# Sparse layer of a fused two-block kernel: order of the input projection, rotary halves packed by DMA, index work placed among the query units

## The reference, cut to what matters

```python
def dsa_mixer(h, w_in, w_out, cos_a, sin_a, cos_i, sin_i):
    proj = h @ w_in
    q, k, v, qi, ki, wi = jnp.split(proj, cuts, axis=-1)   # 16, 4, 4 heads of 64; 8, 1 index heads of 64; 8
    q = partial_rope(q, cos_a, sin_a, 16)                  # the first 16 of 64 features are turned
    k = partial_rope(k, cos_a, sin_a, 16)
    qi = partial_rope(qi, cos_i, sin_i, 16)
    ki = partial_rope(ki, cos_i, sin_i, 16)
    wi = wi * IDX_WEIGHT_SCALE
    def block(i):                                          # 64 queries each
        logits = jnp.einsum('bthd,bsd->bths', qib, ki)
        score = jnp.einsum('bths,bth->bts', jax.nn.relu(logits), wib)
        score = jnp.where(visible[None], score, -jnp.inf)
        _, sel = lax.top_k(score, 64)
        ...                                                # k and v gathered, softmax over the selected keys
    return o @ w_out
```

## Time and profile before

| | us |
|---|---|
| median of 3 executions | 1638.37 |
| lowest, highest | 1637.73, 1640.66 |
| the profiled execution | 1634.39 |
| its span in the trace | 1632.5 |
| granted clock of TensorE in it | 0.999 |

### The profile page before, as it was taken

How to read it: one execution, slowest core, us unless ns; L and a number is a source line. 1 busy time by engine, 2 the same in 40 slices (tenths; PEclk the granted TensorE clock), 3 DMA queues, 4 the chain that set the end, 5 groups by cost and what they waited for, 6 DMA issues and landing times.

```text
span 1632.5 us, 30999 instructions
## 1 busy us (share of the span) xinstructions
PE 1590.4 (97%) x12663; PEld 1517.9 (93%) x12663; DVE 1011.2 (62%) x1241; ACT 763.9 (47%) x1005; POOL 23.5 (1%) x40
## 2 busy tenths in 40 slices
PE   7989999998999999999999999999999999999999
PEld 5969999998999998999988999989999898889998
DVE  7786665567666546566457666466654656676653
ACT  4345554447555444434346444344443435554443
POOL 0000000013000000000000000000000000000000
PEclk9999999999999999999999999999999999999999
DMA  6702666744256664556623556635566352236573
GB/s 164 183 31 58 179 201 181 197 141 123 83 179 202 182 195 153 181 166 194 181 77 104 180 177 195 168 113 174 178 195 189 103 181 78 79 129 196 189 213 96
DMA packets 347111, 252.70 MB, mean 155 GB/s; under 512 B 32622, under 2 KB 345868, under 8 KB 347036
## 3 DMA queue, kind: packets, MB, share of 16 engines
q1 hardware_dynamic: 345424, 250.00, 51.4%
q10 hardware_dynamic: 1612, 1.64, 0.3%
HBM read 250.58 MB, written 1.05 MB: 154 GB/s over the span
## 4 chain that ended last, share of the span: by engine, by line
PE 86%; DVE 8%; ACT 3%; DMA 2%; issue 1%; SPq 0%; ACTq 0%; DVEq 0%
PE acc L541 26%; PE acc L543 25%; PE acc L542 25%; DVE w_low L1690 2%; ACT w_high L1199 1%; PE acc L566 1%; PE acc L771 1%; PE spare L739 1%; DMA w_raw<-in_ffn_w_dram 1%; PE acc L757 1%; DVE x_state L1900 1%; DVE xg_low L1734 1%; DVE evac_a L1898 1%; PE spare L604 1%; PE spare L566 1%
## 5 line engine op out<-in xcount | busy, mean ns | idle before, releaser
L1690 DVE TENSOR_TENSOR w_low<-w_raw,w_high 128x2048 fp32r<-128x2048 f32 (+2 forms) x222 | 528.5, 2381 | 378.3 <-ACT w_high L1199 378.3
L1199 ACT ACTIVATE w_high<-w_raw 128x2048 fp32r<-128x2048 f32 (+2 forms) x222 | 441.3, 1988 | 612.0 <-PE acc L543 578.3
L541 PE MATMUL acc<-xg_high,w_high 128*128 128x272 f32 (+2 forms) x2320 | 663.4, 286 | 7.6 <-DVE xg_low L1734 4.4
L542 PE MATMUL acc<-xg_low,w_high 128*128 128x272 f32 (+2 forms) x2320 | 654.6, 282 | 0.0
L543 PE MATMUL acc<-xg_high,w_low 128*128 128x272 f32 (+2 forms) x2320 | 654.6, 282 | 0.0
L541 PEld LDWEIGHTS acc<-xg_high,w_high 128*128 128x128 f32 (+1 forms) x2320 | 435.5, 188 | 19.4 <-issue 9.4
L542 PEld LDWEIGHTS acc<-xg_low,w_high 128*128 128x128 f32 (+1 forms) x2320 | 435.5, 188 | 2.4 <-issue 1.7
L543 PEld LDWEIGHTS acc<-xg_high,w_low 128*128 128x128 f32 (+1 forms) x2320 | 435.4, 188 | 0.2
L541 PE MATMUL acc<-hidden_high,w_high 128*128 128x256 f32 (+1 forms) x1216 | 342.2, 281 | 2.6 <-DVE w_low L1690 2.6
L542 PE MATMUL acc<-hidden_low,w_high 128*128 128x256 f32 (+1 forms) x1216 | 341.4, 281 | 0.0
L543 PE MATMUL acc<-hidden_high,w_low 128*128 128x256 f32 (+1 forms) x1216 | 341.4, 281 | 0.0
(11 more groups left out here) (297 smaller groups left out, 1441.7 us busy)
## 6 DMA issues: line engine op xcount, KB each, us to landing
w_raw<-in_ffn_w_dram SPq DMA_DIRECT2D x88, 1024.0 KB, 5.1
w_raw<-in_ffn_w_dram SPq DMA_DIRECT2D x32, 1408.0 KB, 6.9
w_raw<-in_mlp_w_up_dram SPq DMA_DIRECT2D x32, 1024.0 KB, 5.7
w_raw<-in_mlp_w_down_dram SPq DMA_DIRECT2D x32, 1024.0 KB, 5.6
w_raw<-in_attn_w_qkv_dram SPq DMA_DIRECT2D x12, 1024.0 KB, 5.0
w_raw<-in_a_w_in_dram SPq DMA_DIRECT2D x18, 256.0 KB, 4.5
w_raw<-in_a_w_in_dram SPq DMA_DIRECT2D x4, 1024.0 KB, 7.7
w_raw<-in_a_w_out_dram SPq DMA_DIRECT2D x4, 1024.0 KB, 5.2
```

Source lines behind the costliest of these rows:

```text
L541: pe.matmul(dst, high_w, high, start=first, stop=False)
L542: pe.matmul(dst, high_w, low, start=False, stop=False)
L1199: act.activation(whi[slot(c)][:, 0:SIZES[c]], raw[c % 2][:, 0:SIZES[c]], ACT.Copy).then_inc(S["w_high"], 1)
L1690: dve.tensor_tensor(wlo[slot(c)][:, s], raw[c % 2][:, s], whi[slot(c)][:, s].bitcast(F32), ALU.subtract)\
```

## The change

- The order of units in `a_in` becomes: two of index queries, index key and weights, v, k, four of queries. The query weights are loaded in two pieces of 128 columns in place of four of 64, and put in the former order by the split (`head_pairs`, two instructions for one on ACT and on DVE).
- `turn_rope` and `rotA` are gone. DVE writes each unit straight to its place (`projected`). ACT then issues DMAs that copy the rotary rows of each head, 8 rows for each half, into a packed tile (`pack`); DVE turns all heads of the group with both halves on the same partitions (`rope_packed`), and ACT issues the DMAs back (`unpack`). There are three groups: index (72 rows), keys with the first eight query heads (96), the other eight query heads (64).
- The value turns come after the unit of k. The logits q = 0 to 3 stand in unit 6 behind k tiles 2 to 5, q = 4 to 7 in unit 7 behind k tiles 1 to 4. Relus and weighing follow among the units, as do seven rounds of the first selection; the eighth stands behind unit 8.
- Filler: 7 products before the value turns are gone, 16 before the masks become 4, and those at pieces 0 and 1 become 2 and 1 in place of 4 and 4.

```diff
 # TensorE
-            turn_rope(g, 0, P, 2, rotA)
...
             wide(g, 2, META, SEQ, tiles=key_and_weights)
-            turn_rope(g, 1, P, 2, rotA)
-            for j in range(3, 7):
-                wide(g, j, META, SEQ)
-                turn_rope(g, j - 1, P, 1 if j == 3 else 2, rotA)
...
+            wide(g, 4, META, SEQ)
+            pe.wait_ge(S["dve_evac"], g.r0 + 4)
+            for i in range(2):
+                for m in range(2):
+                    ins = pe.transpose(sp[0][:, i, m * P:(m + 1) * P], vF[:, m, i * P:(i + 1) * P], ident)
+                ins.then_inc(S["v_turned"], 1)
+            wide(g, 5, META, SEQ)
+            wide(g, 6, META, SEQ, beside=index_logits(0, 2))
+            wide(g, 7, META, SEQ, beside=index_logits(4, 1))
+            wide(g, 8, META, SEQ)
...
+                    if q == 0:
+                        pe.wait_ge(S["idx_back"], 16 * 20)
+                        pe.wait_ge(S["v_ready"], n.add("v_ready", 2))
+                        pe.wait_ge(S["wi_ready"], 1)
+                    if q >= 2:
+                        pe.wait_ge(S["idx_relu"], q - 1)
...
+            def heads_ready(i, m):
+                if i == 0 and m == 0:
+                    pe.wait_ge(S["key_back"], 16 * 2 * len(key_rotary))
+                if i == 0 and m == 4:
+                    pe.wait_ge(S["query_back"], 16 * 2 * len(query_rotary))
 # ACT
+            def pack(j, rotary, to, signal):
+                act.wait_ge(S["dve_evac"], g.r0 + j + 1)
+                for tile, m, c, head in rotary:
+                    for s in range(2):
+                        act.dma_start(pack_rows(to, head, s), head_rows(tile, m, c, s)).then_inc(S[signal], 16)
...
+            split(g.c0 + 5)
+            split(g.c0 + 6)
+            unpack(index_rotary, packI, "idx_roped", "idx_back")
...
+            pack(4, key_rotary[8:], packK, "key_packed")
             copy_v([(sp[0][:, i, 0:KV_COLS], vA[:, i, :]) for i in range(2)])
+            split(g.c0 + 7)
+            pack(5, key_rotary[0:4], packK, "key_packed")
+            relus(0)
+            split(g.c0 + 8)
+            pack(6, key_rotary[4:8], packK, "key_packed")
+            relus(4)
+            split(g.c0 + 9)
+            unpack(key_rotary, packK, "key_roped", "key_back")
+            pack(7, query_rotary[0:4], packQ, "query_packed")
+            split(g.c0 + 10)
+            pack(8, query_rotary[4:8], packQ, "query_packed")
+            def beside_exps(p):
+                if p == 1:
+                    unpack(query_rotary, packQ, "query_roped", "query_back")
 # DVE
+            def rope_packed(pack, rows_, packed, count, roped):
+                dve.wait_ge(S[packed], 16 * count)
+                c, s = tb[0][0:rows_, :, 0:SEQ], tb[1][0:rows_, :, 0:SEQ]
+                dve.tensor_tensor(c, pack[0:rows_], across(cosA[0:rows_], 2), ALU.mult)
+                link(dve.tensor_tensor(s, pack[0:rows_], across(sinA[0:rows_], 2), ALU.mult))
+                dve.tensor_tensor(pack[0:rows_, 0], c[:, 0], s[:, 1], ALU.subtract)
+                dve.tensor_tensor(pack[0:rows_, 1], c[:, 1], s[:, 0], ALU.add).then_inc(S[roped], 1)
...
+            projected(3, vF[:, 0:2, 0:SEQ], 2)
+            split(g.c0 + 5)
+            rope_packed(packI, IDX_ROWS, "idx_packed", 18, "idx_roped")
...
+            weigh(0)
+            projected(6, qA[:, 2:4, :], 2, A_SCALE)
+            split(g.c0 + 8)
+            take_eight(0, 3)
+            weigh(4)
+            projected(7, qA[:, 4:6, :], 2, A_SCALE)
+            split(g.c0 + 9)
+            rope_packed(packK, KEY_ROWS, "key_packed", 2 * len(key_rotary), "key_roped")
+            take_eight(0, 4)
+            projected(8, qA[:, 6:8, :], 2, A_SCALE)
+            split(g.c0 + 10)
+            take_eight(0, 1)
```

More of the change, by code:

```diff
@@ L70 @@
 C_INVB = C_INVA + 1
-C_RA = C_INVB + 1
-C_RB = C_RA + P
+C_RB = C_INVB + 1
 C_CHUNK = C_RB + P
@@ L724, in turn_values, with attention @@
                     ins.then_inc(S["v_turned"], 1)
-            def attention(pieces, scores, prob_tiles, values, probs_by, idle=(), early=0, values_in=0, mask=None):
+            def attention(pieces, scores, prob_tiles, values, probs_by, idle=(), early=0, values_in=0, mask=None, before=None):
                 s0, t0, o0, e0 = n.get("s_read"), n.get("pt_ready"), n.get("o_read"), n.get("exp_done")
@@ L735, in make_scores @@
                 def make_scores(p):
+                    if before is not None:
+                        before(*pieces[p])
                     if p >= 2:
@@ L1372, in copy_v, with attention @@
                     act.activation(d, pieces, ACT.Copy).then_inc(S["v_ready"], 1)
-            def attention(pieces, keys, slots, outs, first=None):
+            def attention(pieces, keys, slots, outs, first=None, beside=None):
                 s0, t0, o0 = n.get("s_read"), n.get("pt_full"), n.get("o_full")
@@ new lines, in unpack, with relus @@
+            def unpack(rotary, src, roped, signal):
+                act.wait_ge(S[roped], 1)
+                for tile, m, c, head in rotary:
+                    for s in range(2):
+                        act.dma_start(head_rows(tile, m, c, s), pack_rows(src, head, s)).then_inc(S[signal], 16)
+            def relus(first):
+                for q in range(first, first + 4):
+                    act.wait_ge(S["idx_full"], q + 1)
+                    if q >= 2:
+                        act.wait_ge(S["idx_read"], q - 1)
+                    nk = (q // 4 + 1) * P
+                    act.activation(Sm[q % 2][:, :, 0:nk], sp[q % 2][:, :, 0:nk], ACT.Relu).then_inc(S["idx_relu"], 1)
```

181 lines of the change are left out of this document (104 added, 77 removed).

## The result

| | before | after |
|---|---|---|
| median of 4 executions, us | 1638.05 | 1705.28 |
| lowest, highest | 1637.39, 1640.66 | 1695.27, 1710.43 |
| the profiled execution | 1634.39 | 1707.18 |
| its span | 1632.5 | 1705.3 |
| granted clock in it | 0.999 | 0.963 |

The change makes the kernel slower by 4.03% (ratio 1.0403, 95% interval 1.0381 to 1.0426): 67.2 us by the medians, 72.8 by the two spans. The forecast was slower, 1646.9, with a range to 1659. The direction held and the size did not, by eight times.

A forecast was written before the change was run, and what follows sets the result against it. TensorE was taken to bound the input projection, then the chain to the first softmax piece. The terms 6.6 - 0.9 + 0.3 + 1.0 + 1.5 gave +8.5 us, median 1646.9, range 1634 to 1659.

The forecast's parts named there:

- ledger: Event-by-event timeline from unit 2 to the third softmax piece at 0.36 us per issue: that piece 6.6 us later.
- price of an issue: ACT's sequencer time per 8-row DMA: 0.36 us taken, ends 0.30 and 0.47, below them zero; 118 make 42 us.
- Step 1 to step 3: Savings: rotary turns off TensorE 6.4 us; logits, value turns, weighing out of the tail 7.6; selection rounds among units 5.0.
- some 20: Before the softmax: its start would come some 20 us sooner if the change added nothing.
- The slope given: Each hundredth of a microsecond per issue is worth 0.8 us, some 80 of 118 issues lying on the path.
- +1.0: On ACT's queue: issues beside SyncE's own 1 MB issues cost 0.9 more, one on the path, +1.0 us.
- the prediction's own figures for 0.43: Issue price estimated from the skill's 512 sequencer cycles at 1.2 GHz; the ledger would then say 1655 us.
- clock term: TensorE idle from 84.9 to 97.1 and sparse until 114 lowers the granted clock: +1.5 us, bounds 0 and 5.
- the smaller terms: Added to the ledger's 6.6: DVE's selection lead -0.9, split chunks +0.3, issues beside SyncE's +1.0, clock +1.5 us.
- Dearer issues: Rival on ACT's queue: no overlap with activations gives 1650 us, 0.48 us an issue gives 1657; chance 0.20.
- Cheap issues: Rival on ACT's queue: below about 0.26 us an issue the kernel gets faster, 1632 at 0.20; chance 0.15.
- the draw: Rival: at 0.27 to 0.31 us an issue the third piece slips 0 to 2.7, total within 3.3 us; chance 0.15.

The follow-up runs named there:

- half-issue kernel: The changed kernel with every second of its 118 small DMAs left out, 59 remaining, rotary output not the reference's: 1672.5 us, ratio 1.0215.
- the kernel with no DMA at all: The changed kernel without its 118 DMAs and the packed turns on DVE, so without any rotary part: 1646.7 us, ratio 1.0045.
- the filler kernels: The changed kernel, all issues kept, with unread filler products in TensorE's waits: 1689.9 us; with the middle two groups cut, 1681.9 us.

## Why the prediction was right in its direction and wrong in its size

| step | predicted | ledger with 0.66 | measured |
|---|---|---|---|
| price of an issue | 0.36 | 0.66 | 0.66 |
| TensorE idle in unit 6 | 3.8 | | 11.8 |
| unit 8 ends | 84.9 | 99.0 | 105.9 |
| keys' rows are back | 97.1 | 118.1 | 123.8 |
| masks | 103.2 | | 133.0 |
| third softmax piece | 114.5 | 142.7 | 150.1 |
| attention, longer by | 1.5 (clock) | | 22.5 |

**Right:** that 118 issues of ACT's own sequencer would cost more than the change saves, that they overlap with activations, and where the waits fall: in unit 6 behind the index rows, after unit 8 for the keys' rows, at the second chunk's split, and between the second and third piece for the 16 returns. All four are in the trace. A fifth wait was missed, the 2.8 us ahead of unit 3: with "unit 2 ends at 41.7 as before; unit 3 at 47.3" the first packs were taken to hold nothing up, and at 0.66 they do. Step 1 to step 3, what the change takes away, can't be read one by one; together with free turns they brought 7.6 us (with fillers) to 12.9 at the third piece, where "some 20" was said without anything added. That figure had not been followed through DVE and the clock.

**The first failed step is the price of an issue.** "I take 0.36, the like-sized row" rested on rows whose source was DRAM. The prediction said that no row copies SBUF to SBUF and widened the bounds only downwards, to zero; upwards it stopped at 0.47, the dearest undisturbed row of the wrong kind. The measured price is twice the row. The Trainium skill (DMA: Bandwidth & Descriptors, Why a DMA increments its semaphore by 16 and not by 1) led to an estimate of 0.43; the trace says 0.63, so that estimate was short too, though on the right side of 0.36. The rule of the Trainium skill that the time to initiate a DMA is usually small relative to the DMA itself (DMA: Bandwidth & Descriptors, Issuing engines are not separate DMA queues) did not carry over to 118 of them in a row, as the prediction said; here they were the largest single cost. Worked through again with 0.66 for each issue and nothing else changed (20 index returns 13.2 us instead of 7.2, 24 of the keys 15.8 instead of 8.6, the last 16 10.6 instead of 5.8, and the first eight packs now ahead of the split for unit 3), the ledger gives +34.8 us at the third piece instead of +6.6. The slope given, 0.8 us per hundredth, was too flat for so long a way: 28.2 / 30 = 0.94, since with dearer issues more of the 118 come to lie on the path. The half-issue kernel, whose queue is as long as 118 issues of 0.33 would make it, bears the ledger out to within 5 us. Two smaller things of the same step: "+1.0" for issues beside SyncE's was not needed, as none of the 118 took more than 0.75 us; and the prediction's own figures for 0.43 don't agree, since 0.8 us per hundredth gives 1652.5 and not 1655.

**The second failed step is the clock term**, "+1.5, bounds 0 and 5". It was sized from a lull of 2 us whose clock came back within two stretches, behind which TensorE ran dense products; the stretch from 14 to 16 between them, which the rows leave out, was half idle too (1.05 us busy of 2). Among the units of the projection the clock did come back as it did there, even behind 11.8 us of waiting. The step that failed is to take the same for what stands behind the masks, the attention. Its cost was 22.5 us, fifteen times the term and over four times its upper bound. This part would have been there at 0.36 an issue as well: the kernel with no DMA at all had it. The prediction also left out that the change takes fillers away, which stood in the list of the change. With the forecast's issue price and this clock the sum is 8.5 - 1.5 + 22.5 = 29.5, 1668; with the real price and the forecast's clock it is 34.8 + 1.9 = 36.7, 1675 (1.9 being the smaller terms with their clock). Either error alone puts the time above the range.

**What is left.** 42.3 - 34.8 = 7.5 us at the third piece are in neither. Nearly all of it, 6.9, is there when unit 8 ends (105.9 for 99.0). An estimate from the rows: the busy time of TensorE at the low clock among the units, from 44.67 to 49, 78 to 82 and 90 to 102, loses 1.6 + 2.0 + 2.9 = 6.5 us against full clock. In the half-issue kernel, which has 5 us of the same, it is the stretches from 66 to 70 and 70 to 78, TensorE busy throughout at 0.50 and 0.69, which lose 2.0 + 2.5 us. So the size fits the clock; it is argued and not shown, as the filler kernels pay for their fillers in the same place. The +8.0 of the rest is 8.0 in this pair of executions only, and the later stage at 0.88 is an estimated 4 of them (0.12 of 35.07). By the medians the whole is 67.2, that is 5.6 less, and kernels with unchanged code there vary by as much.

**The rivals.** "Dearer issues" was the nearest, for its mechanism, but its end was 0.48, and its 1657 carried 1.5 us for the clock. "Cheap issues" and the draw fall with the first row of the timeline.

## What to carry to other kernels

Price a DMA by a row that has the same source and destination memory, and where there is none, keep the upper bound as open as the lower. Count issues on a compute engine's queue as work of that engine for everything that stands behind them in order. When a change opens a wait of TensorE ahead of a stretch of short products, price the whole stretch at half the clock as a case of its own, and fill the wait with products that end before the data arrive.

## What the runs showed of the hardware

- An issue with its source in SBUF holds the issuing sequencer for 0.63 us, from DRAM 0.32 (ACT, destination SBUF). On SyncE it is 0.62 from SBUF; from DRAM five of eight took 0.30 to 0.37 and three 0.61 to 0.62. From SBUF one row, 8, 16 or 64 rows make little difference (medians 0.61 to 0.64).
- The scores that waited for the returned rows of keys start 1.3 us after the last of these issues ended (122.45 to 123.76), where 2.3 was taken for the landing.
- ACT's sequencer goes on issuing while an activation runs (split at 40.37 for 1.92 us, issues from 40.40).
- Granted clock 0.50 (1.2 GHz) through 49 us in which TensorE was busy 48.24, through 40.00 of 40 and 47.73 of 48 in others, all with float32 products of 64 to 256 columns; at 1.00 (2.4 GHz) the same products hold it (42.28 busy us of 43). In one execution, of the kernel before without its fillers, they won it back at 110. A busy TensorE in the profile is no sign that the clock will rise, and what makes it rise in the attention stays open.
- Behind a wait of 2.8 us the clock was 0.50 for the next 2.3 us of the projection, and 1.00 again from 49 on; behind one of 11.8 us 0.50 from 78 to 82, then 1.00.
